# Expert gate and up weights loaded four rows per partition, with the contraction index permuted to match

## The reference, cut to what matters

```python
def hier_moe(x, w_group, b_group, w_inner, b_inner, w_gate, w_up, w_down):
    gl = einsum('btd,dg->btg', x, w_group) + b_group
    pg = softmax(gl); gval, gidx = top_k(pg, 1)
    il = einsum('btd,dge->btge', x, w_inner) + b_inner
    ...                       # softmax inside the chosen group, top 2, gates
    h = silu(einsum('btd,edf->btef', x, w_gate)) * einsum('btd,edf->btef', x, w_up)
    h = h * gates[..., None]
    return einsum('btef,efd->btd', h, w_down)
# x (1, 256, 1024), w_gate and w_up (2, 16, 1024, 256), w_down (2, 16, 256, 1024)
```

## Time and profile before

| | |
|---|---|
| three runs | 966.77, 967.99, 972.16 us |
| profiled execution, span of its instructions | 960.3 us |
| TensorE matmuls busy | 871.0 us, 91% |
| TensorE weight loads busy | 734.5 us, 76% |
| VectorE, ScalarE, GpSimd busy | 612.3, 440.7, 73.1 us |
| DMA | 145.00 MB, 97725 packets |

### The profile page before, as it was taken

One profiled execution on the slowest core, in us unless ns is written; L12 is line 12 of the kernel. 1 busy time (PEld: TensorE's weight loads), 2 busy tenths in 40 slices (PEclk: granted clock), 3 DMA queues, 4 the chain that ended last, 5 costly groups with the idle time before them and its releaser, 6 DMA issues.

```text
span 960.3 us, 13095 instructions
## 1 busy us (share of the span) xinstructions
PE 871.0 (91%) x5181; PEld 734.5 (76%) x5181; DVE 612.3 (64%) x725; ACT 440.7 (46%) x466; POOL 73.1 (8%) x96
## 2 busy tenths in 40 slices
PE   2999899999999998889999997899678889999995
PEld 1757689897998977787877875889555787787874
DVE  4949764524734237547898897545572548788886
ACT  3455223240132404426666576443571427666673
POOL 9401320000100000000000000000021000000000
PEclk8999999999999999989999999999897999999999
DMA  9714520000000002707898988255200709898891
GB/s 240 279 63 135 176 72 1 1 1 1 1 1 1 1 1 88 241 1 245 290 334 285 323 300 282 83 183 175 88 1 0 263 1 309 300 316 298 286 329 46
DMA packets 97725, 145.00 MB, mean 151 GB/s; under 512 B 4745, under 2 KB 70449, under 8 KB 97665
## 3 DMA queue, kind: packets, MB, share of 16 engines
q1 hardware_dynamic: 96848, 142.28, 43.8%
q0 software_dynamic: 816, 1.90, 0.9%
HBM read 143.11 MB, written 1.05 MB: 150 GB/s over the span
## 4 chain that ended last, share of the span: by engine, by line
PE 71%; DVE 17%; ACT 5%; issue 4%; DMA 2%; POOL 0%; DVEq 0%; SPq 0%; POOLq 0%; ACTq 0%
PE ps L1577 13%; PE ps L1579 12%; PE ps L1578 12%; DVE w_lo L960 4%; PE ps L1737 4%; PE ps L1561 4%; PE ps L1749 3%; PE ps L1947 3%; DVE w_lo L1100 2%; PE ps L1763 2%; PE ps L1710 2%; PE ps L1620 1%; ACT w_hi L602 1%; PE ps L1995 1%; ACT ps L613 1%
## 5 line engine op out<-in xcount | busy, mean ns | idle before, releaser
L960 DVE TENSOR_TENSOR w_lo<-w_ring,w_hi 128x2048 fp32r<-128x2048 f32 x80 | 183.0, 2300 | 62.5 <-PE ps L1579 59.8
L602 ACT ACTIVATE w_hi<-w_ring 128x2048 fp32r<-128x2048 f32 x80 | 152.9, 1915 | 133.6 <-PE ps L1579 115.8
L1100 DVE TENSOR_TENSOR w_lo<-w_ring,w_hi 128x2048 fp32r<-128x2048 f32 x48 | 109.2, 2287 | 6.1 <-PE ps L1579 5.8
L660 ACT ACTIVATE w_hi<-w_ring 128x2048 fp32r<-128x2048 f32 x48 | 92.0, 1917 | 37.5 <-PE ps L1579 37.5
L1577 PE MATMUL ps<-w_hi,xe_hi 128*128 128x512 f32 x256 | 102.8, 402 | 5.9 <-DVE xe_lo L1118 2.9
L1578 PE MATMUL ps<-w_lo,xe_hi 128*128 128x512 f32 x256 | 100.6, 393 | 0.0
L1579 PE MATMUL ps<-w_hi,xe_lo 128*128 128x512 f32 x256 | 100.5, 393 | 0.0
L1577 PE MATMUL ps<-w_hi,xa_hi 128*128 128x512 f32 x160 | 66.6, 416 | 15.0 <-DVE xa_lo L1272 8.8
L1561 PE MATMUL ps<-ident 128*128 128x128 f32 x488 | 66.5, 292 | 4.5 <-issue 2.9
L1391 DVE TENSOR_TENSOR w_lev<-ps,level 128x512 f32<-128x512 f32 x40 | 27.7, 692 | 62.5 <-PE ps L1737 62.5
L1561 PEld LDWEIGHTS ps<-ident 128*128 128x128 f32 x488 | 61.8, 205 | 6.5 <-issue 4.0
(11 more groups left out here) (336 smaller groups left out, 1698.6 us busy)
## 6 DMA issues: line engine op xcount, KB each, us to landing
w_ring<-in_moe_w_gate_dram SPq DMA_DIRECT2D x64, 512.0 KB, 3.9
w_ring<-in_moe_w_up_dram SPq DMA_DIRECT2D x64, 512.0 KB, 4.9
w_ring<-in_moe_w_down_dram SPq DMA_DIRECT2D x64, 512.0 KB, 4.9
w_ring<-in_rw_w_rkv_dram SPq DMA_DIRECT2D x24, 512.0 KB, 5.9
w_ring<-in_w_kv_dram SPq DMA_DIRECT2D x16, 512.0 KB, 4.9
w_ring<-in_rw_w_out_dram SPq DMA_DIRECT2D x8, 512.0 KB, 6.4
w_ring<-in_sb_w_q_dram SPq DMA_DIRECT2D x8, 512.0 KB, 4.3
w_ring<-in_sb_w_out_dram SPq DMA_DIRECT2D x8, 512.0 KB, 4.3
```

The lines of the kernel that those rows point to most:

```text
L602: nc.scalar.activation(whi[n % HI][:, :, :], w_ring[n % RING][:, :, :], ACT.Copy).then_inc(hi_ready, 1)
L660: nc.scalar.activation(whi[n % HI][:, :, :], w_ring[slot][:, :, :], ACT.Copy).then_inc(hi_ready, 1)
L960: nc.vector.tensor_tensor(wlo[n % LO][:, :, :], w_ring[n % RING][:, :, :], whi[n % HI][:, :, :].bitcast(f32), ALU.subtract).then_inc(lo_re ...
L1100: nc.vector.tensor_tensor(wlo[n % LO][:, :, :], w_ring[n % RING][:, :, :], whi[n % HI][:, :, :].bitcast(f32), ALU.subtract).then_inc(lo_re ...
```

## The change

Each gate or up load now takes four consecutive rows per partition: partition p holds rows 4p to 4p+3 of the half, 4 KB adjacent in memory and adjacent in `w_ring`. In a slot, gate fills the first 1024 floats of the partition and up the last 1024, so the matmul's moving operand for block i is two runs of 256 floats, 1024 floats apart, where it was one run of 512. Block b of the contraction now means columns 4c + (b mod 4) of the half, c from 0 to 127. So the transposes of the expert phases' norm and the gather read their stationary operand with a step of 4 floats (16 bytes) through the new `by_rows`, and the router weights are loaded in the same order, in twice as many DMAs.

```diff
@@ def gate_up (SP) @@
-                    sp.dma_start(w_ring[slot][:, :, a * F:(a + 1) * F],
-                                 src.rearrange("(b p) f -> p b f", p=P)).then_inc(w_loaded[slot], 16)
+                    sp.dma_start(w_ring[slot][:, 2 * a:2 * a + 2, :],
+                                 src.rearrange("(p q i) f -> p q (i f)", p=P, q=2)).then_inc(w_loaded[slot], 16)
@@ router weights (POOL) @@
-                pool.dma_start(wr[k][:, :, 0:G], moe_w_group[k].rearrange("(b p) g -> p b g", p=P)
-                               ).then_inc(router_loaded, 16)
-                pool.dma_start(wr[k][:, :, G:NR], moe_w_inner[k].rearrange("(b p) g e -> p b (g e)", p=P)
-                               ).then_inc(router_loaded, 16)
+                for h_ in range(2):
+                    pool.dma_start(wr[k][:, 4 * h_:4 * h_ + 4, 0:G],
+                                   moe_w_group[k, h_ * HALF:(h_ + 1) * HALF].rearrange("(p i) g -> p i g", p=P)
+                                   ).then_inc(router_loaded, 16)
+                for h_ in range(2):
+                    pool.dma_start(wr[k][:, 4 * h_:4 * h_ + 4, G:NR],
+                                   moe_w_inner[k, h_ * HALF:(h_ + 1) * HALF].rearrange(
+                                       "(p i) g e -> p i (g e)", p=P)).then_inc(router_loaded, 16)
@@ moe_phase (ACT) @@
-                    act.wait_ge(router_loaded, 16 * 8)
+                    act.wait_ge(router_loaded, 16 * 12)
@@ TensorE @@
+            def by_rows(t, j, b):
+
+                g, i = b // 4, b % 4
+                return t[:, j, g * HALF:(g + 1) * HALF].rearrange("p (c i) -> p i c", i=4)[:, i, :]
+
-            def norm(nm):
+            def norm(nm, rows=False):
...
-                                                xs[:, j, b * P:(b + 1) * P], ident[:, :])
+                                                by_rows(xs, j, b) if rows else xs[:, j, b * P:(b + 1) * P],
+                                                ident[:, :])
...
-                norm(nm)
+                norm(nm, True)
@@ gather @@
-                                                 x_[:, j, b * P:(b + 1) * P], pick[:, j, :],
+                                                 by_rows(x_, j, b), pick[:, j, :],
@@ gate_up, in packed_experts and in all_experts @@
-                    wh, wl = whi[n % HI], wlo[n % LO]
+                    wh = whi[n % HI][:, :, :].rearrange("p (a q) (i f) -> p (q i) a f", a=2, i=2)
+                    wl = wlo[n % LO][:, :, :].rearrange("p (a q) (i f) -> p (q i) a f", a=2, i=2)
```

## The result

| | before | changed kernel |
|---|---|---|
| median of 4 runs | 967.76 us (966.77 to 972.16) | 1024.19 us (1017.98 to 1027.03) |
| profiled execution, span | 960.3 us | 1025.0 us |
| ratio of times, 95% interval | | 1.0556 (1.0514 to 1.0598) |

The change makes the kernel 56.4 us slower. The forecast was 992.2 us, its range ended at 1002: the sign is right, the size is not, and the time lies outside the range.

The account below looks back on a forecast made before the run. The prediction took TensorE to bound the kernel, with the gather bound by its weight loads. Its terms, −0.5 + 24.6 + 0.1 = +24.2 us, on 968.0 gave 992.2 us, range 966 to 1002.

Parts of the forecast that it names:

- the gather's term: In the gather, 256 stationary loads with a 16-byte step take 0.208 us in place of 0.112: +24.6 us.
- a doubling: Upper bound for the gather: the distance between its loads doubles, 256 x 0.112 = +28.7 us.
- Hidden transfers: Expert phases' gate and up loads: 4 KB runs are worth nothing where TensorE covers the loads.
- −0.5: At moe1's start, a faster load shortens ScalarE's 1.09 us wait: −0.5 us.
- The two-run moving operand as nothing: In gate_up, 768 matmuls read their moving operand in two runs: taken as nothing, 1.3 us as a bound.
- The transposes' +0.1: In the expert phases' norm, strided transposes cost +0.096 us a load in moe0, mostly covered, and 0 in moe1: +0.1 us.
- The masks: At POOL, 4 more DMAs move the masks' end to 40.6 us, before TensorE's piece at 69.09: 0.
- The free step: Rival: the gather's step costs TensorE nothing, only the transfer's gain is left, 967.5 us; chance 0.24.
- the share: Rival: the gather's step costs a share, 1.57 times the load distance, 0.176 us, +16.4 us, so 983.9 us; chance 0.13.
- the faster kernel: Rival: half of TensorE's 13.8 us idle in the expert stretches goes with 4 KB runs, 961.1 us; chance 0.08.
- The clock case: Rival: the granted clock also falls behind each of 8 gathers, 8 x 1.7 = 13.6 us, so 1005.8 us; chance 0.10.

Follow-up runs that it names:

- the wide gather: The changed kernel with each gather matmul reading `pick` four times over as moving operand, 512 columns: 999.87 us, ratio 1.0341.
- step 2: The kernel before with the gather reading its stationary operand with a step of 2 floats (8 bytes): 968.48 us, ratio 0.9992.
- step 4 with 512 columns: Stretch of a separate kernel without the trunk: float32r matmuls, stationary step 4 floats, 512 moving columns; one every 0.236 us, against 0.227 for a dense one.
- the 64-column gather: The kernel before with 64 moving columns in place of 128 in each gather matmul, stationary operand adjacent: 980.54 us, ratio 1.0156.
- the gather's step alone: The kernel before with only the gather's stationary read changed to a step of 4 floats: 1024.19 us, ratio 1.0589.
- all but the gather's step: The changed kernel with the gather reading adjacent columns again: 968.27 us, ratio 1.0006.
- the kernel of its own: A separate kernel without the trunk, profiled once: stretches of matmuls behind dense ones, with varied operand steps and widths; loads 0.113 us apart at step 1, 0.232 at step 4.

## Why the prediction was wrong in size

**The step that failed** is the gather's term, "256 x 0.096 = +24.6 us", and with it the decision to keep the clock out of the sum. The load's term measures 30.7 to 31.4 us, and the clock's, which stood at nothing, 21 to 24. Both errors point the same way.

The load. VectorE's 1.63 ns a float gave 0.208 us for 128 of them; the trace has 0.2345, 1.83 ns a column. 256 x (0.2345 − 0.112) = +31.4 us; the chain's gathers say +30.7, the wide gather +30.8. The step was to price TensorE's load by a VectorE instruction, on the premise that the memory takes the same time for a float whoever asks; the row of 32 floats came near by luck, since the same 16 bytes cost a transpose's load 0.01 to 0.02 us and a bfloat16 load 0.007. The bound "a doubling", 28.7, was taken for an upper end without a row that made it one, and it fell too. The direction and the reason held: the gather is bound by its loads, and step 2 (+1.5 us in the chain) and step 4 with 512 columns (0.236 against 0.227) show when a slow load is seen and when it is hidden. The loads over the steps go 0.113, 0.119, 0.185, 0.232, 0.240. By that the rule of the Trainium skill, SBUF — State Buffer, section Specifications (TRN2), is borne out for float32 matmuls: two hits in a 16-byte line read at nearly full rate (0.119 us with step 2), one hit does not (0.232 with step 4, 0.223 with step 5). The transposes' 0.123 and bfloat16's 0.062 at one hit a line differ from it, and there the measurement decides.

The clock. The forecast gave it a chance of 0.10 and "8 x 1.7 = 13.6" us; it came, and cost 24.3 by the medians, 3.0 a gather. Its ground against it was that the clock is 0.99 and 1.00 over the stretches with the gathers of before. But those gathers put 128 columns into 0.112 us, and the question was what 128 columns in 0.21 do. That the case was near is shown by the 64-column gather: at before's own pace of loads that kernel is 11 us slower. The price failed since the earlier trace rows show a fall where 12 matmuls ran at 0.61 on average, behind a stretch (425.7 to 429.4) in which TensorE was busy only 2.24 of 3.70 us. Here the clock is down to 0.50 before the gather ends, and all twelve matmuls of the down piece come every 0.43 us instead of 0.23. The distances of the gathers give it. From the second gather on they are 48.0 us against 45.4 in the wide version: 2.5 to 2.7 us, four times, 10.3 in all. The first distance of each phase is 45.3 and 45.5 against 42.1 and 42.5, 6.2 in the two together. Behind the start of moe1's last gather the changed kernel runs on for 66.4 us and the wide one for 63.7, 2.6 more. If moe0's last gather costs 2.6 as well, that makes 21.7. The 2.6 that are missing to 24.3 may be no cost at all: the ratios leave room for them, and the stretch from moe0's last gather to moe1's first differs between executions by as much (251.0 us in the changed kernel, 247.8 with the gather's step alone).

**The rest of the sum** holds. Hidden transfers: all but the gather's step is 1.0006 (0.9967 to 1.0044). "−0.5" at moe1's start: the wait went from 1.09 to 0.62 us. The two-run moving operand as nothing: 32 such matmuls come every 0.227 us in the kernel of its own, as dense ones do. The transposes' +0.1 measures 0, and its working was wrong: each load was to cost 0.096 more and costs 0.02. The masks end at 40.4 us and TensorE's first piece behind them starts at 69.02, against 69.09 in the earlier trace rows: 0. The two terms, 30.8 + 24.3 = 55.1 us, are the two legs of one difference (1024.19 − 969.10), so that they come near the 56.4 of the medians proves nothing. The account from the chains alone, 30.7 + 21.7 = 52.4, does test it: the interval of the ratio is 50 to 58 us. Of the 64.7 us between the two spans, the 9.6 above 55.1 are mostly the runs' own: 2.8 + 5.5 by which the two profiled executions lie on either side of their medians. Part of that stands in `rwkv`, which the change does not touch.

**The rivals.** The free step (0.24) fell with the gather alone, the share (0.13) with 0.2345 against its 0.176, the faster kernel (0.08) with 1.0006. The clock case was the nearest, and true together with the forecast's mechanism, not in place of it. The sum with both terms as measured would have read 968.0 − 0.5 + 31.4 + 24.3 = 1023.

## What to carry to other kernels

A layout that gives the DMA longer runs hands its stride to whoever reads the operand. Before it is made, look at which side pays: in float32 and float32r matmuls a stationary operand read 16 bytes apart costs twice the load here (0.232 us for 0.113), and where the moving operand has only 128 columns nothing hides it. And when loads set the pace of a row of narrow matmuls, price the granted clock too, by what stands behind them: one experiment with a wider moving operand tells the two apart. Here a step of two floats keeps the longer runs (2 KB) without either cost, and the gain is nothing all the same, because the transfers were hidden from the start.

## What was not expected of the hardware

The granted clock fell while the matmul side was busy without a gap: with 128 columns every 0.232 us (0.74 over the stretch) and with 64 every 0.121 (0.91), but not with 256 every 0.234 (1.00); all these are float32r, and plain float32 with 128 columns every 0.232 kept 1.00. More multiplying made the program 24.3 us faster by the medians.

The moving operand minds its step earlier than the stationary one. With 512 columns and a step of two floats a matmul takes 0.45 us instead of 0.227, and with four floats 0.458:

```profile
L77 PE MATMUL ps<-mv,xr x32: 615/630/637, 152.3 to 166.3; 128*128 128x512 f32 x32
...
L80 PE MATMUL ps<-mv,xr x32: 622/639/639, 173.6 to 187.8; 128*128 128x512 f32 x32
```

A load in the weight path of a transpose doesn't double with 16 bytes (0.123 us), while one of a float32 matmul of the same data does (0.232).
